# Two transformer blocks in float32 on one core: where the learned tokens stand in the third block's operand, and six filler matmuls ahead of four stretches

## What is computed

```python
# first block, twice
h = _layernorm(x) * (1.0 + scale) + shift
u_f, z_f, cq, ckv, k_r, z_a = jnp.split(h @ w_in[l], split_pts, axis=-1)
y_f = _fourier_mix(u_f, w_fmix[l]) * jax.nn.silu(z_f)
y_a = _mla_attention(q_nope, q_rope, k_nope, k_rope, v) * jax.nn.silu(z_a)
x = _layernorm(ALPHA * x + gate * (jnp.concatenate([y_f, y_a], -1) @ w_out[l]), ln_g[l], ln_b[l])
# second block: 16 learned tokens stand ahead of the 256
h = jnp.concatenate([meta_b, x], axis=1)
proj = rms_norm(h, g_pre_mix) @ w_in_2
z_pool, v_conv, g_conv, gate_a, gate_b = jnp.split(proj, splits, axis=-1)
y_a = causal_multiscale_pool(z_pool, w_pool_grp, pool_scale) @ w_pool_out
y_b = conformer_conv(v_conv, g_conv, w_dw, b_dw, conv_ln_g, conv_ln_b) @ w_conv_out
m = jax.nn.sigmoid(gate_a) * y_a + jax.nn.sigmoid(gate_b) * y_b
h = h + rms_norm(m @ w_o, g_post_mix)
f = jnp.square(jax.nn.relu(rms_norm(h, g_pre_mlp) @ w_up)) @ w_down
h = h + rms_norm(f, g_post_mlp)
return h[:, 16:]
```

## Time and profile before

| | before |
|---|---|
| median of 3 runs | 2041.43 us |
| the runs | 2040.3, 2041.43, 2044.02 us |
| the profiled execution's own time | 2043.44 us |
| its span, first to last instruction | 2041.8 us |
| PE busy | 1995.0 us, 98% |
| DVE, ACT busy | 1378.0 us (67%), 923.2 us (45%) |
| granted TensorE clock, mean | 0.997 |
| HBM traffic | 458.45 MB read, 226 GB/s over the span |

### The profile page before, as it was taken

The page is one execution under the profiler, slowest core; times in us unless marked ns, Lnnn a source line. Parts: engine busy times, 40 slices in busy tenths (PEclk is TensorE's granted clock), DMA queues, the critical chain, the costliest instruction groups (busy, mean ns, idle before and its releaser), DMA issues.

```text
span 2041.8 us, 36334 instructions
## 1 busy us (share of the span) xinstructions
PE 1995.0 (98%) x14157; PEld 1816.7 (89%) x14157; DVE 1378.0 (67%) x1882; ACT 923.2 (45%) x1372; POOL 34.0 (2%) x67
## 2 busy tenths in 40 slices
PE   6999999999999999999999999999999999999998
PEld 2789888789999988999999998899899889989986
DVE  5458887785788758889997555655455545555546
ACT  3344455354545544434354344464344334434443
POOL 0000000000000000000000000000000000000000
PEclk9999999999999999999999999999999999999999
DMA  9988888855587753455445555545555555555553
GB/s 376 410 339 326 304 343 341 344 228 186 190 307 269 287 210 143 167 185 178 173 167 215 195 185 194 218 159 191 198 187 186 191 191 181 195 194 185 185 195 135
DMA packets 64983, 462.06 MB, mean 226 GB/s; under 512 B 7328, under 2 KB 7872, under 8 KB 9328
## 3 DMA queue, kind: packets, MB, share of 16 engines
q1 hardware_dynamic: 56576, 401.71, 53.1%
q0 software_dynamic: 8304, 58.90, 7.7%
HBM read 458.45 MB, written 2.13 MB: 226 GB/s over the span
## 4 chain that ended last, share of the span: by engine, by line
PE 72%; DVE 5%; ACT 1%; issue 0%; DVEq 0%; ACTq 0%
PE ps L660 24%; PE ps L661 24%; PE ps L662 24%; DVE w_lo L1917 2%; DVE area L1954 1%; PE ps L705 0%; DVE X L2471 0%; DVE grow L2572 0%; DVE area L2572 0%; ACT w_hi L1344 0%; DVE st L1937 0%; PE ps L1097 0%; DVE y_lo L1937 0%; DVE X L2448 0%; DVE area L2672 0%
## 5 line engine op out<-in xcount | busy, mean ns | idle before, releaser
L1917 DVE TENSOR_TENSOR w_lo<-raw,w_hi 128x1024 fp32r<-128x1024 f32 (+2 forms) x650 | 745.8, 1185 | 382.7 <-ACT w_hi L1344 380.8
L1344 ACT CAST w_hi<-raw 128x1024 fp32r<-128x1024 f32 (+3 forms) x650 | 630.7, 1019 | 456.2 <-PE ps L662 454.7
L660 PE MATMUL ps<-a,w_lo 128*128 128x256 f32 (+1 forms) x2912 | 823.7, 283 | 5.0 <-DVE w_lo L1917 2.0
L662 PE MATMUL ps<-a,w_hi 128*128 128x256 f32 (+1 forms) x2912 | 815.9, 280 | 0.0
L661 PE MATMUL ps<-a,w_hi 128*128 128x256 f32 (+1 forms) x2464 | 689.3, 280 | 0.0
L660 PEld LDWEIGHTS ps<-a,w_lo 128*128 128x128 f32 x2912 | 547.6, 188 | 28.9 <-issue 23.5
L662 PEld LDWEIGHTS ps<-a,w_hi 128*128 128x128 f32 x2912 | 551.0, 189 | 0.0
L661 PEld LDWEIGHTS ps<-a,w_hi 128*128 128x128 f32 x2464 | 463.4, 188 | 0.6 <-issue 0.5
L660 PE MATMUL ps<-w_hi,y_lo 128*128 128x512 f32 x720 | 281.3, 391 | 0.0
L661 PE MATMUL ps<-w_lo,y_hi 128*128 128x512 f32 x720 | 280.4, 389 | 0.0
L662 PE MATMUL ps<-w_hi,y_hi 128*128 128x512 f32 x720 | 280.3, 389 | 0.0
(11 more groups left out here) (310 smaller groups left out, 2034.8 us busy)
## 6 DMA issues: line engine op xcount, KB each, us to landing
raw<-in_stream SPq DMA_DIRECT2D x328, 1024.0 KB, 4.8
area<-in_ada POOLq DMA_DIRECT2D x48, 1024.0 KB, 6.4
area<-in_ada SPq DMA_DIRECT2D x38, 1024.0 KB, 8.7
grow<-in_ada SPq DMA_DIRECT2D x10, 1024.0 KB, 7.3
area<-in_rows POOLq DMA_DIRECT2D x4, 1024.0 KB, 5.0
raw<-in_stream SPq DMA_DIRECT2D x7, 384.0 KB, 6.2
X<-in_x SPq DMA_DIRECT2D x1, 2048.0 KB, 7.9
grow<-row_scratch POOLq DMA_DIRECT2D x2, 1024.0 KB, 8.2
```

The lines of the kernel that those rows point to most:

```text
L660: pe.matmul(o, w[1], a[0], start=first, stop=False, skip_group_check=shared)
L662: return pe.matmul(o, w[0], a[0], start=False, stop=last, skip_group_check=shared)
L1344: ac.copy(to, raw[:, bass.ds((g % RAW) * CH + at, n)]).then_inc(hi_ready, 1)
L1917: ve.tensor_tensor(to, raw[:, bass.ds((g % RAW) * CH + at, n)], hi.bitcast(F32), ALU.subtract).then_inc(lo_ready, 1)
```

## The change

It has two parts. **The learned tokens** move from the 16 columns ahead of the tokens to the 16 columns behind them. The operand with 272 columns then begins where the tokens begin, at 192 modulo 256 bytes. `pad` and `pool_z` are still to hold the learned tokens first, so the two instructions that fill them are now two each, one for 256 columns and one for 16. **The fillers**: `settle()` issues six matmuls of `lat_hi` against itself, 128 stationary and 256 moving columns, into PSUM bank 7, which nobody reads. It stands ahead of the loop over the gate_b and branch chunks and ahead of the second, third and fourth `up`: four times in an execution, 24 matmuls.

```diff
-        def wide_tile(e, k, lo=0, n=T):
+        def wide_tile(e, k, n=T):
             t, i = (st, k - KT // 2) if e and k >= KT // 2 else (a_both, e * KT + k)
-            at = i * WIDE + WIDE_AT + SHIFT + lo
+            at = i * WIDE + WIDE_AT + SHIFT
             return t[:, at:at + n]
...
-            return t[:, at:at + n * WIDE].rearrange("p (k t) -> p k t", k=n)[:, :, SHIFT - META:SHIFT]
+            return t[:, at:at + n * WIDE].rearrange("p (k t) -> p k t", k=n)[:, :, SHIFT + T:SHIFT + TM]
...
             def am_ops(k):
-                return wide_tile(0, k, -META, TM), wide_tile(1, k, -META, TM)
+                return wide_tile(0, k, TM), wide_tile(1, k, TM)
...
+            def settle():
+
+                for _ in range(6):
+                    pe.matmul(bank(7), lat_hi[:, 0:P], lat_hi[:, 0:T], start=True, stop=True)
...
+            settle()
             with pe.Fori(AHEAD, KT // 2) as i:
                 for b in range(2):
                     gate_b(i, b)
...
             with pe.Fori(1, FF_BLOCKS - 1) as f:
+                settle()
                 with pe.Fori(0, KT // 2) as i:
                     for b in range(2):
                         up(f, i, b, False)
                 down(f, False, False)
             f = FF_BLOCKS - 1
+            settle()
             with pe.Fori(0, KT // 2) as i:
...
-                ac.copy(pool_z, bank(2, 0, TM)).then_inc(pl_in, 1)
+                ac.copy(pool_z[:, META:TM], bank(2))
+                ac.copy(pool_z[:, 0:META], bank(2, T, META)).then_inc(pl_in, 1)
...
-                ve.scalar_tensor_tensor(out=pad[:, ahead:ahead + TM], in0=th[:, :], scalar=1.0, in1=bank(0, 0, TM),
-                                        op0=ALU.add, op1=ALU.mult).then_inc(cv_in, 1)
+                for to, at, n in ((ahead + META, 0, T), (ahead, T, META)):
+                    o = ve.scalar_tensor_tensor(out=pad[:, to:to + n], in0=th[:, at:at + n], scalar=1.0,
+                                                in1=bank(0, at, n), op0=ALU.add, op1=ALU.mult)
+                o.then_inc(cv_in, 1)
```

## The result

| | before | after |
|---|---|---|
| median | 2041.43 us | 2032.98 us |
| runs | 5, 2040.3 to 2048.34 | 5, 2031.52 to 2037.62 |
| the profiled execution, its span | 2043.44, 2041.8 us | 2037.62, 2035.9 us |
| granted TensorE clock, mean | 0.997 | 0.996 |

The ratio is 0.9948, with a 95% interval of 0.9932 to 0.9965. By the medians the change is faster by 8.5 us, by the ratio by 10.6, where 18.4 were forecast. The measured median lies 10 us above the predicted one. The profiled execution of after is the slowest of its five.

What follows compares the result with a forecast made beforehand. PE, with 72% of the chain of waits, was taken as the bound through its matmul spacing. +3.0 - 14.6 - 6.8 = -18.4 us from the median 2041.43 gave 2023.0 us, range 2020 to 2032.

Steps and rivals of the forecast that it cites:

- The fillers: Gate loop and up: four filler places cost +3.0 us; 3264 matmuls at the close spacing save 14.6 us.
- Rivals 3: Fillers reset nothing, only the operand's new start counts: -3.8 us, 2037.6 us; chance 0.07.
- 4: Neither part works, one distance per width, fillers only take time: 2044.6 us; chance 0.06.
- 5: Slower: waits alone set the spacing; gate loop, up and 256-column mix-tile matmuls wide: +6.7, 2048.1 us; chance 0.05.
- 6: Fillers work at some places only, two of four: about -11, near 2030 us; chance 0.03.
- 272 columns at 192: Mix tiles: 1152 matmuls of 272 columns take 120.0 instead of 126.7 ns, -7.7 us; bounds 120.0 and 133.3 ns.
- Rival 1: Start does not matter for 272 columns, so only the fillers gain: -11.3, 2030.1 us; chance 0.22.
- The gate_a chunks: Mix tiles: the 256-column chunks between the 272-column streams stay at 113.3 ns.
- Rival 2: Mix tiles go wide, entered at a first-tile wait: +1.2 instead of -6.8; with fillers -10.4, 2031.0 us; chance 0.12.
- -6.8 were to arrive: Mix tiles: of the 7.7 us saved by the operand's new start, 6.8 us reach the total time.
- DVE and ACT: Mix tiles: DVE's split instruction costs 0.15 us more, ACT's second copy at most 0.22 us.
- The lateness of 0.2 us: Last mix tile: DVE's 0.88 us wait for PE turns into 0.2 us late, lost on DVE's path.

## Why the prediction was right in its sign and not in its size

**The fillers: right to a tenth.** Forecast +3.0 and -14.6, together -11.6 us. The traces have -3.5 in the gate loop and -8.0 behind the first `up`, together -11.5. The places cost 0.74 us each, the gate loop and the last three `up` ran at 113.3 ns. Fillers alone gave the whole measured gain. Rivals 3, 4, 5 and 6 fell with this. The Trainium skill (page "TensorE: Matmul & The Clock Gate", section "Back-to-back issue gap") gives columns / 2.4 + 2.5 ns; it calls this the gap of an isolated matmul, not that of a stream with a weight load for each matmul, as here, and it says nothing of addresses. As an estimate by that formula 256 columns take 109.2 ns and 272 take 115.8. Here 256 columns stand 113.3 to 120.0 ns apart by start and run-up, and 272 columns 123.3 to 126.7: no stream of either width came down to its figures.

**272 columns at 192: the step that failed.** "I take 120.0" was the cheap one of my two bounds, reached by counting periods over the columns at three points of which none was 272 at 192. It is 123.3. Of the 6.7 ns a matmul that I expected, half came: 1152 x 3.4 = -3.9 us in place of -7.7. The bound of 120.0 was no bound from a row of that width at all. Rival 1, that the start does not matter for 272 columns, fell too: moving it took 3.4 ns off each of them. Its time of 2030.1 us was nearer to the measured one than mine all the same.

**The gate_a chunks: the second half of the same step.** I left them at 113.3 ns. They went to 117.8, 768 x 4.5 = +3.5 us. Rival 2 had this, with a chance of 0.12: -2.5 + 3.5 + 0.2 for the tiles (the 272-column spacing at 124.5 where it is 123.3) and 2031.0 us in all. It is the case that happened, but not by its mechanism: it had an entry at a wait, which fillers would have cured, where the 272-column stream at 192 leaves a wide one behind by itself, at every tile. My own text held the clue, that 126.7 ns streams "are always followed by close ones"; I used it for a rival and not for the sum. Together the mix tiles gave -0.4 us (-0.6 and +0.2 in the table) where -6.8 were to arrive.

**DVE and ACT: the terms were small, and smaller still.** In the trace of after the two pieces of the multiplication stand as

```profile
1028.87 0.50 DVE L2613 SCALAR_TENSOR_TENSOR rs<-th,ps 128x256 f32<-128x256 f32 x2 [0.83 <-ACT th L1703]
```

0.50 us for both where one took 0.44: 0.06 and not 0.15. ACT's two copies took 0.37 and 0.18 us where one took 0.39, 0.17 more, within the 0.22 that I allowed. DVE's wait ahead of them, 0.83 us against 0.88, did not go, since the tiles came no sooner. The lateness of 0.2 us that I charged for never arose.

**The first `up`: what was not in the sum.** I took its close spacing for granted ("113.3 ns in the gate loop and in all four `up`"), since it ran close in the trace of before. In the nine traces without fillers there it was close in three (before, tokens alone, fillers in every tile) and wide in six. The same code, two fillers everywhere, came to its fillers wide in one execution and close in another. It is decided at a short delay, not by the transposes: in seven of the fourteen traces the twelve matmuls right behind the last transposes have the other spacing than the rest of the `up`. After them PE waits twice for the operand that DVE is still normalising (`ln_lo` in `two_chunks`), and the spacing behind the second of these waits stays to the end of the `up` or to its fillers. That second delay, in the trace of before:

```profile
1333.57 0.28 PE L662 MATMUL ps<-a,w_hi 128*128 128x256 f32 x1
1333.68 0.37 PE L660 MATMUL ps<-a,w_lo 128*128 128x256 f32 x1
1333.88 0.28 PE L661 MATMUL ps<-a,w_hi 128*128 128x256 f32 x1
```

The distance of the last two starts was 193 or 194 ns in two traces and 205 or 206 in four, all close behind it; 195 in three, 200 in three and 220 in two, all wide behind it. So what seems to count is the moment at which DVE delivers, to a nanosecond or a few. This was read afterwards and no run sets that moment: it is where to look, not a shown cause. The change alone does not decide it, since with the tokens behind it was close in two traces (tokens alone, fillers in every tile) and with the tokens ahead wide in one (fillers alone). It cost the profiled execution 3.1 us. All four profiled executions of the changed program, with or without a tail, had it wide, so it may weigh on the median too; why it falls so often this way was not tried.

**The numbers.** -11.5 for the fillers and -0.4 for the tiles make -11.9; the wide first `up` brings it to some -8.9. The median moved by -8.5; that these agree is in part luck, since how often the first `up` is wide in either kernel is not known. In the profiled executions the start of the program, slower by 2.8 us in after, and 0.3 up to the mix tiles leave the -5.9 of the spans. The range ended at 2032 and the median was 2032.98 (2041.43 x 0.9948 is 2030.8): with rival 2 at 2031.0 I had put the edge too near to it, and had left out that a stretch which nobody sets, 3 us of first `up` and some 2 us in layer 2's in-projection, can fall either way in either kernel.

## What to carry to other kernels

When an engine never waits, read the distances of its instructions by width, start and what ran ahead, before and behind each edge; a stream's price may be paid by the one that follows it. A value that no row shows is better measured in a tail of a few dozen matmuls than reasoned from its neighbours: here one such tail would have shown 123.3 ns and the loss behind it. And a reset has to be tried from each state that it can meet: two fillers looked as good as six until they met a close stream.

## What the runs showed of the hardware that was not expected

- At the full granted clock (1.00 in all stretches shown) 256 moving fp32r columns have two lasting spacings at the start 192 modulo 256 bytes, 113.3 and 117.8 ns. Behind a 256-column stream, two matmuls of 256 columns at 0 swapped them (eight of eight) and six set the close one (nine of nine gate loops and first `up`, five of which came in wide and four close); behind 512 columns two, three, six or twelve set the close one, and one leaves the wide one.
- 272 columns at 128 leave the close spacing behind them, at 192 the wide one, with no wait between.
- The spacing changes with the start in steps of 16 bytes: 113.3 ns at 192, 117.3 at 160, 119.2 at 176 and 208, 118.3 at 224 for 256 columns, each behind two fillers. It is not even in the width: 240 columns took 112.0 ns, only 1.3 less than 256, while 264 took 6.7 more.
- The same code takes one or the other spacing in different executions at a delay behind transposes, which makes 3 us in a first `up` and 2 us in layer 2's in-projection (some 470 x 4.5 ns). That this is part of the spread of the kernel's runs is likely, not shown.
